# Attention scores that may open one step after the end of the unit three in front

## The reference

```
score = where(key chunk <= query chunk, sum_h relu(qi_h . ki) * wi_h, -inf)
idx   = top_k(score, 256)                       # sparse choice of keys
logits = (q . k[idx]) * 64**-0.5 + rel_bias[t5_bucket(pos(idx) - qpos)]
p = softmax(logits);  o = p . v[idx]            # 16 heads, 4 key/value heads, head size 64
y_a = (o * silu(g_attn)) @ w_attn_out
```

## Time and profile before

| | |
|---|---|
| median of 3 runs | 3454.37 us (3446.77 to 3455.05) |
| profiled execution | 3443.51 us, of which the span shown is 3441.8 us |
| PE busy over the span | 3251.4 us (94%) |
| DVE, ACT, POOL busy | 78%, 43%, 30% |
| attention, first phi to last phi | 1853.17 to about 2804 us: 951 us |
| PE, DVE, ACT busy in it | 865.65, 823.33, 627.31 us |

### The profile page before, as it was taken

The page is one execution under the profiler, slowest core; times in us unless marked ns, Lnnn a source line. Parts: engine busy times, 40 slices in busy tenths (PEclk is TensorE's granted clock), DMA queues, the critical chain, the costliest instruction groups (busy, mean ns, idle before and its releaser), DMA issues. The chain is left out here.

```text
span 3441.8 us, 50403 instructions
## 1 busy us (share of the span) xinstructions
PE 3251.4 (94%) x19461; PEld 2993.3 (87%) x19461; DVE 2688.7 (78%) x4071; ACT 1465.9 (43%) x1961; POOL 1036.0 (30%) x888
## 2 busy tenths in 40 slices
PE   7999999999999999999997898898998989999998
PEld 4999888999999999999996777777777779989987
DVE  2443789989999999999996898898888865886444
ACT  2322567988820100010005676666676640433121
POOL 3322112443335300000003443543433324664200
PEclk9999999999999999999999999999999999999999
DMA  6455435455555643454443323223122235567443
GB/s 239 128 183 174 142 106 155 150 172 178 179 185 181 256 154 136 142 170 158 160 157 100 83 56 86 67 58 90 48 62 57 57 131 183 187 226 256 131 146 113
DMA packets 381524, 485.53 MB, mean 141 GB/s; under 512 B 49296, under 2 KB 304464, under 8 KB 379685
## 3 DMA queue, kind: packets, MB, share of 16 engines
q1 hardware_dynamic: 325605, 287.14, 28.1%
q10 hardware_dynamic: 44352, 149.49, 12.4%
q0 software_dynamic: 11392, 46.68, 3.4%
HBM read 301.98 MB, written 184.13 MB: 141 GB/s over the span
## 5 line engine op out<-in xcount | busy, mean ns | idle before, releaser
L1140 PE MATMUL psum<-ha,gt 128*128 128x352 f32 x8136 | 1350.9, 324 | 6.8 <-DVE ha L1414 4.4
L1140 PEld LDWEIGHTS psum<-ha,gt 128*128 128x128 f32 x8136 | 1320.8, 188 | 10.7 <-DVE ha L1414 4.7
L1450 DVE SCALAR_TENSOR_TENSOR cv<-cv,vecs,cv 128x1056 f32<-128x1056 f32 (+1 forms) x480 | 607.8, 1359 | 0.0
L1924 ACT CAST at<-psum 128x1024 fp32r<-128x1024 f32 (+2 forms) x308 | 288.7, 937 | 314.9 <-PE psum L1835 314.4
L1998 DVE TENSOR_TENSOR at<-psum,at 128x1024 fp32r<-128x1024 f32 (+2 forms) x308 | 346.1, 1128 | 79.5 <-ACT at L1924 77.6
L1835 PE MATMUL psum<-ident,at 128*128 128x128 f32 (+1 forms) x2320 | 342.5, 273 | 40.8 <-ACT at L1905 30.4
L1854 PE MATMUL psum<-at,at 128*128 128x512 f32 (+1 forms) x1160 | 340.4, 396 | 27.3 <-ACT at L1932 26.9
L1835 PEld LDWEIGHTS psum<-ident,at 128*128 128x128 f32 (+1 forms) x2320 | 272.4, 141 | 103.4 <-ACT at L1905 37.7
L717 PE MATMUL psum<-br,br 128*128 128x352 f32 x2016 | 338.6, 329 | 14.8 <-DVE br L2371 9.3
L717 PEld LDWEIGHTS psum<-br,br 128*128 128x128 f32 x2016 | 332.1, 191 | 18.6 <-issue 10.4
L1271 ACT ACTIVATE gt<-psum 128x1056 f32<-128x1056 f32 x80 | 84.0, 1049 | 599.8 <-PE psum L1140 599.8
(11 more groups left out here) (255 smaller groups left out, 4126.2 us busy)
## 6 DMA issues: line engine op xcount, KB each, us to landing
scratch_ws<-gt SPq DMA_DIRECT2D x112, 512.0 KB, 4.0
gt<-scratch_ws ACTq DMA_DIRECT2D x110, 512.0 KB, 5.0
gt<-in_w_in_dram SPq DMA_DIRECT2D x60, 512.0 KB, 5.7
scratch_gm<-gt ACTq DMA_DIRECT2D x32, 528.0 KB, 3.0
br<-scratch_gm ACTq DMA_DIRECT2D x32, 528.0 KB, 3.8
scratch_m<-br POOLq DMA_DIRECT2D x32, 528.0 KB, 5.4
at<-scratch_q SPq DMA_DIRECT2D x128, 128.0 KB, 2.9
scratch_u<-gl POOLq DMA_DIRECT2D x16, 528.0 KB, 4.2
```

Source lines behind the costliest of these rows:

```text
L1140: return nc.tensor.matmul(of[:, j, 0:W // 3], part[:, c, :], a[:, c, j * (W // 3):(j + 1) * (W // 3)], start=(c == 0 and k == 0), stop=(c ...
L1450: ins = nc.vector.scalar_tensor_tensor(to[:, 0:width], mine[:, k_:k_ + width], tap, to[:, 0:width], ALU.mult, ALU.add)
L1924: nc.scalar.copy(phi[j % 3][:, 0:len(mine), 0:n], turned[j % 2][:, 0:len(mine), 0:n]).then_inc(s_phi, 1)
```

## The change

One expression in the planner. `opens` was last[u-3] + 3, or first[u] - 7 where that is earlier, but never before last[u-3] + 1; now it is always last[u-3] + 1.

```diff
@@ AttentionPlan.__init__ @@
         for item, by in zip(items, latest):
             u = item[0]
-            opens = max(self.last[u - 3] + 1, min(self.last[u - 3] + 3, self.first[u] - 7)) if u >= 3 else self.begin
+            opens = self.last[u - 3] + 1 if u >= 3 else self.begin
             while step < opens or (step < by and seen >= (3 if step % 3 == 0 else 2)):
                 step, seen = step + 1, 0
```

## The result

The changed kernel takes 3414.03 us (median of 4 runs, 3411.43 to 3415.91) against 3452.34 us (3446.77 to 3455.05): ratio 0.9891, 95% interval 0.9873 to 0.9908, so 32 to 44 us faster. The forecast was 30 us less than before, 3424 us, from 3402 to 3447 us.

What follows compares the result with a forecast made beforehand. PE was taken to be held up by ACT in attention, with DVE close behind. Turn 24.8, copy 20.9 and clock 8, less 6 for POOL, made 47.7 us, cut to 30: 3454.4 - 30 = 3424 us, range 3402 to 3447.

Steps and rivals of the forecast that it cites:

- What bounds: Attention stage: PE is busy 865.7 of 951.1 us, DVE close behind; PE's two largest matmul waits are on ACT.
- Turn waits: PE's turns (L1835) waiting for exponentials (L1905): 30.4 us falls to 5.6, a gain of 24.8 us.
- Copy waits: PE's value products (L1854) waiting for ACT's copy (L1932): 26.9 us falls to 6, a gain of 20.9 us.
- all 16.7 us go: Claim that the eight copy waits of 1.5 us or more, summing to 16.7 us, vanish entirely.
- Clock: Five low-clock stretches in the attention stage cost at most 9.7 us; 8 us of that was counted as gain.
- POOL and the masks: POOL's order stays the same; folds (L1979) colliding with POOL rise from 11 to 17, a loss of 6 us.
- The sum: 24.8 + 20.9 + 8 - 6 = 47.7 us, cut to 30 for DVE; trusted stage bound 919 us.
- DVE did not take over: Rival: PE's waits for ACT become waits for DVE; gain falls to 0 to 10 us, 3444 to 3454; chance 0.12.
- The slower case: Rival: folds beside POOL's subtractions (L1763) each lose up to 0.9 us; 14 us slower, 3468 us; chance 0.05.
- chunks would stand earlier and still wait: Rival: chunks still wait for queries or a ring bank; gain 17 or 10 us, 3437 to 3444 us; chance 0.14.
- The signs: Turn waits 4 to 9 us, copy 4 to 10, phi under 45, at most one low-clock stretch, attention 915 to 930.
- signs of being wrong: PE's waits for L1964, L1979, L1998 up over 20 us, L1979's mean over 0.9, or new copy waits over 1.5.

Runs made afterwards that it cites:

- The kernel with the short units alone: Kernel before, with the new opening only for short units (t = 0 to 7), long units and sample opening as before: 3432.07 us, ratio 0.9936.
- The experiment on the copy alone: Kernel before, with ACT's copy of the finished unit (L1932) placed ahead of its step's exponentials instead of behind them: 3437.43 us, ratio 0.9962.
- with the loads earlier: Changed kernel, with the next group's key, value and bias loads issued on SP nine steps earlier: 3397.97 us, ratio 0.9852.
- the two experiments that take it away in different ways: Changed kernel with group loads nine steps earlier, 3397.97 us; or with late loads but POOL's seven pieces of group preparation one unit later, 3394.0 us.
- that of the earlier loads in the kernel before: Kernel before, with the next group's loads issued nine steps earlier: 3450.92 us, ratio 0.9997.
- the same edit: Changed kernel with earlier group loads and the softmax-sum division (L1979) on ACT: 3428.69 us; with PE's turn back one step later, 3379.82 us.

## Why the prediction was right, and which terms were off

*What bounds.* Right: PE's waits for ACT at the unit borders were the time to be had, and filling empty steps took most of it. The kernel with the short units alone, in which unit borders are filled and copies are not, has half of the turn waits and all of the copy waits.

*Turn waits.* Forecast 30.4 to 5.6 us, measured 12.5. The 2.8 us places lost theirs in three of four groups (1.43 us stays in the third), the 1.2 us places keep 0.3 to 0.6 us. At the groups' borders 1.4 to 1.7 us of 2.1 stay, where I had 0.9, and of the 1.4 us places 0.7 to 1.0 in three groups. The term was mis-sized because it priced every chunk as one of 512 columns, 0.55 us. At the groups' borders the two chunks are of 256 columns and cost PE 0.56 us together (2087.56 to 2088.12), not 1.1:

```profile
2087.56 0.36 PE L1819 MATMUL psum<-at,at 128*128 128x256 f32 x1
2088.12 0.64 PE L1854 MATMUL psum<-at,at 128*128 128x256 f32 x4
2090.40 0.66 PE L1835 MATMUL psum<-ident,at 128*128 128x128 f32 x4 [1.65 <-ACT at L1905]
```

At the first 1.4 us place they are three of 384 columns, 1.3 us together, and the wait fell by 0.4 us only. Before, PE had also waited 0.51 us just ahead of it for the plo, and that went too; the rest isn't accounted for.

*Copy waits.* Forecast 6 us left, measured 7.7. Of the eight large ones five went as a whole and two fell to 0.75 us; the one of 2.87 us kept 1.36, so that "all 16.7 us go" was 2.9 us too much. The experiment on the copy alone adds what the sum had to guess: 26.9 us of these waits were worth 13 us of time in the kernel before.

*Clock.* Forecast 8 us of gain. The five stretches went, and each of the three new stalls brought one of its own, 8.2 us of missing shares of which 5.8 us fall on time with PE busy; with the loads earlier only the stretch at the stage's start is left. That short waits and low clock go together held for the stretches that went, but most of the term was lost to a stall that the sum hadn't got. It also rested on one trace: that of the earlier loads in the kernel before, with the scores placed as before, has eight such stretches in the stage and 15 us of missing shares.

*POOL and the masks.* This is the step that failed. It said that POOL's order is the same and priced only collisions at L1979, 6 us of loss. POOL's order is the same, but what it waits for in that order isn't: before, its wait for the value load was short (1.4 to 2.4 us in the three groups) and hidden, and I looked at mask and query loads and not at the group's. That cost some 16 us: the two experiments that take it away in different ways find 16 and 18 us by the medians, 15 and 19 by the stages. The collisions themselves fell: ten L1979 are stretched to over 0.6 us instead of twelve, the longest is 1.09 us instead of 2.39, and the stretching sums to 6.0 us instead of 10.7, so that the term was a gain of some 5 us and not a loss of 6. Counting equal steps in the plan didn't foretell it.

```profile
L1979 DVE TENSOR_TENSOR at<-at,at x68: 418/426/1090, 1870.6 to 2778.4; 128x256 f32<-128x256 f32 x64, 64x256 f32<-64x256 f32 x4
```

*The sum.* The gross sum of 47.7 us was cut to 30 for DVE's sake, with 919 us as the bound I trusted for the stage. The stage came out at 917 us, and that is luck: it is 902 and 898 us without the stalls, 49 to 53 us below before. So the bound was 17 to 21 us too cautious, DVE did not take the part that I had cut for it, and the unseen stall nearly filled the difference. The medians moved by 38 us, with 34 us shown in the stage's traces; the rest is within the scatter of the runs.

*The rivals.* DVE did not take over in this change: it stands idle for phi 37 us less. Of what is left, work taken from DVE gains eight tenths of its length. The slower case, POOL's subtractions beside the fold, did not come. That chunks would stand earlier and still wait was true in three places, for POOL, by way of near masks and queries, as the rival had it, but behind a load that it hadn't named.

*The signs.* Copy waits (7.7 us), DVE's for phi (40.4) and the stage's length (917) lie in the ranges named. The turn waits (12.5 us against 4 to 9) and the stretches of low clock (four against at most one) don't. None of the signs of being wrong came: PE's waits for L1979 hardly moved, those for L1998 grew by 1 us with the 5.83 us stall in them, and L1979's mean fell from 0.58 to 0.52 us. One copy wait, at 2299.58 us, is 1.64 us long, but it is an old one, 1.25 us before, behind the sample's exponentials.

## What to carry to other kernels

When work is moved earlier on one engine, list for each helper engine not only its order but the loads that its next pieces wait for: a wait that was covered by a gap becomes a stall as soon as the gap is filled, and it can be mended by a load issued some steps earlier. A wait that is removed can be worth less than its length where the next engine is nearly as full: 26.9 us of copy waits taken away by a swap on ACT gave 13 us. Spreading ACT's exponentials gave 49 us of the stage once the stalls were gone: PE waits 38 us less for ACT, DVE waits 36 us less for phi, and 8.5 us less of clock is missing. Price each chunk by its own width, not by the largest. When work is given to another engine, look in which step its consumer stands: the same edit was 31 us slower or 18 us faster by one step.

## What the runs showed of the hardware

The stretches of low clock are not tied to the kernel one to one. The kernel before had five in its traced run, behind waits of PE of 2.0 to 2.9 us, and waits of the same lengths in other places were followed by none; with its group loads moved and its waits otherwise the same it had the same five and three more. The changed kernel has one that begins in or just behind each of the three stalls, of 4.6 to 6.1 us, in both of its traces. The issue of one DMA from the cached values (1024 rows of 64 floats at a stride) occupied SP's queue for 7.7 to 8.8 us in the changed kernel, against 0.6 us for the prompt's values (2048 such rows, at a stride too); no run tried why. A product of DVE with both inputs in SBUF (L1979) takes 0.43 us, and 2.39 us in the longest case, beside a POOL subtraction; in the changed kernel eight of the ten stretched ones take 1.05 to 1.09 us.
